# Stick-breaking attention taken two heads at a time, with the mask added ahead of the softplus

## The reference, cut to what matters

```python
z = einsum('bqhd,bshd->bhqs', qb, k) * HEAD_DIM ** -0.5
before = pos[None, :] < pb[:, None]                 # key position below query position
log_one_minus = where(before, log_sigmoid(-z), 0.0)
log_stick = cumsum(log_one_minus, axis=3, reverse=True) - log_one_minus
a = where(before, exp(log_sigmoid(z) + log_stick), 0.0)
o = einsum('bhqs,bshd->bqhd', a, v)
y = (o * silu(g)) @ w_out
```

## Time and profile before

| | |
|---|---|
| time, median of 3 executions | 1088.21 us (1086.91 to 1091.32) |
| span of the profiled execution, first to last instruction | 1090.5 us |
| PE busy | 1050.6 us (96%) |
| DVE, ACT, POOL busy | 700.0, 539.2, 226.2 us (64%, 49%, 21%) |
| PE's mean granted clock | 0.982 of 2.4 GHz |
| DMA | 173.28 MB, mean 159 GB/s |
| first logits product (L581) to first product of `ob` (L361) | 328.80 to 374.94 us |

### The profile page before, as it was taken

How to read it: one execution, slowest core, us unless ns; L and a number is a source line. 1 busy time by engine, 2 the same in 40 slices (tenths; PEclk the granted TensorE clock), 3 DMA queues, 4 the chain that set the end, 5 groups by cost and what they waited for, 6 DMA issues and landing times.

```text
span 1090.5 us, 19954 instructions
## 1 busy us (share of the span) xinstructions
PE 1050.6 (96%) x8160; PEld 1012.0 (93%) x8160; DVE 700.0 (64%) x1002; ACT 539.2 (49%) x822; POOL 226.2 (21%) x167
## 2 busy tenths in 40 slices
PE   8969999999999999999999999999999999999996
PEld 8969986999998899979999999999999999999996
DVE  5989976674446567635555657845566655657843
ACT  4335556355548636445435436644345545436641
POOL 3745201220003423000100202521015100202520
PEclk9889999999999999999999999989999999999998
DMA  9334530646542153624452545446545452545431
GB/s 344 114 117 151 194 116 1 232 154 231 189 161 76 65 192 118 245 102 155 172 174 79 194 158 189 154 166 254 198 171 201 173 188 80 193 159 188 154 116 39
DMA packets 26624, 173.28 MB, mean 159 GB/s; under 512 B 2880, under 2 KB 5184, under 8 KB 5952
## 3 DMA queue, kind: packets, MB, share of 16 engines
q1 hardware_dynamic: 24832, 161.26, 41.4%
q10 hardware_dynamic: 1728, 11.14, 2.6%
HBM read 167.15 MB, written 5.24 MB: 158 GB/s over the span
## 4 chain that ended last, share of the span: by engine, by line
PE 76%; DVE 11%; ACT 5%; POOL 2%; issue 2%; DMA 1%; SPq 0%; POOLq 0%; DVEq 0%; ACTq 0%
PE bank L361 64%; DVE wl L1142 4%; PE bank L467 3%; PE bank L494 2%; DVE work L1453 2%; ACT wh L718 2%; DVE work L1172 2%; DMA vec<-vecs 1%; POOL acc L1579 1%; PE bank L483 1%; DVE work L1456 1%; PE bank L429 1%; PE bank L581 1%; ACT work L1063 1%; PE bank L645 1%
## 5 line engine op out<-in xcount | busy, mean ns | idle before, releaser
L1142 DVE TENSOR_TENSOR wl<-raw,wh 128x1024 fp32r<-128x1024 f32 x300 | 394.6, 1323 | 250.8 <-ACT wh L718 248.9
L718 ACT ACTIVATE wh<-raw 128x1024 fp32r<-128x1024 f32 x300 | 312.9, 1054 | 307.1 <-PE bank L361 289.5
L361 PE MATMUL bank<-xh,wh 128*128 128x256 f32 x1312 | 368.5, 288 | 7.7 <-DVE wl L1142 5.7
L361 PE MATMUL bank<-xh,wl 128*128 128x256 f32 x1312 | 363.8, 284 | 0.0
L361 PE MATMUL bank<-xl,wh 128*128 128x256 f32 x1312 | 340.0, 284 | 0.0
L361 PEld LDWEIGHTS bank<-xh,wh 128*128 128x128 f32 x1312 | 253.2, 193 | 9.1 <-DVE wl L1142 8.1
L361 PEld LDWEIGHTS bank<-xh,wl 128*128 128x128 f32 x1312 | 253.3, 193 | 0.2
L361 PEld LDWEIGHTS bank<-xl,wh 128*128 128x128 f32 x1312 | 238.7, 193 | 0.1
L361 PE MATMUL bank<-yh,wh 128*128 128x256 f32 x768 | 212.3, 289 | 0.9 <-ACT yh L1067 0.9
L361 PE MATMUL bank<-yh,wl 128*128 128x256 f32 x768 | 210.1, 286 | 0.0
L361 PE MATMUL bank<-yl,wh 128*128 128x256 f32 x768 | 180.8, 286 | 4.2 <-POOL yl L1614 4.2
(11 more groups left out here) (154 smaller groups left out, 1320.8 us busy)
## 6 DMA issues: line engine op xcount, KB each, us to landing
raw<-w SPq DMA_DIRECT2D x149, 1024.0 KB, 4.8
k_scratch<-kt ACTq DMA_DIRECT2D x2, 1024.0 KB, 7.2
kt<-k_scratch ACTq DMA_DIRECT2D x2, 1024.0 KB, 6.3
cs<-cst SPq DMA_DIRECT2D x1, 1152.0 KB, 13.0
raw<-w SPq DMA_DIRECT2D x2, 512.0 KB, 5.8
h<-xt SPq DMA_DIRECT2D x1, 1024.0 KB, 6.1
v<-memt ACTq DMA_DIRECT2D x1, 1024.0 KB, 8.3
m_scratch<-yh ACTq DMA_DIRECT2D x1, 1024.0 KB, 4.3
```

The source lines that it names most:

```text
L361: return pe.matmul(b[:, j, :], lhs, rhs, start=k0 + k == 0 and q == 0 and (j == 0 or not both_open), stop=k0 + k == KT * p.deep - 1 and q ...
L718: act.activation(wh[:, n % 2, :, part], raw[:, n % RAW_SLOTS, :, part], ACT.Copy).then_inc(hi_ready, 1)
L1142: dve.tensor_tensor(wl[:, n % 2, :, part], raw[:, n % RAW_SLOTS, :, part], wh[:, n % 2, :, part].bitcast(F32), ALU.subtract).then_inc(lo_r ...
```

## The change

The change does seven things.

1. The logits use 64 rows of the array: `kt[r, g, ...]` and `qz[r, a, ...]` with r the 64 partitions of the head, instead of 128 rows with zeros. The two heads of a pair are issued alternately, each into a bank of its own, and four banks are used in turn instead of two.
2. The three value products of a pair are issued alternately too: first part of both heads, second of both, third of both. They are issued once both heads' Exp is done.
3. TensorE's program goes by pairs: scores of pair g, values of pair g-2, sums of the two heads of pair g-1. Its waits for the banks and for the copy of `v` stand ahead of the scores of pair 1. The hook in `vb` issues the scores of pair 0 together, and the second hook is gone.
4. VectorE adds the mask of -1e30 to the logits first (`z_first`), for a head as soon as its logits are there. ScalarE's Abs reads that masked tile from SBUF and waits for it.
5. The softplus is made from the masked tile (`z_soft` on VectorE), so that a masked place gives 0 by itself. GpSimd's multiplication goes, and the mask of ones and zeros goes from the table of constants: 384 of 2304 columns of 128 x 4 bytes, 192 KB.
6. ScalarE's Exp of the exponent takes head t-4 in step t instead of t-3, VectorE's exponent head t-4 instead of t-2, and the gates have a lag of 8.
7. GpSimd's low parts follow one another with nothing between.

```diff
-            def z_scores(a):
-                if a >= 2:
-                    pe.wait_ge(z_neg, a - 1)
-                b = bank[4 + a % 2]
-                pe.matmul(b[:, 0:S], kt[:, a // 2, 0:P], qz[:, a, :], start=True, stop=True)
-                pe.matmul(b[:, S:S + P], kt[:, a // 2, LATE], qz[:, a, LATE], start=True, stop=True).then_inc(z_full, 1)
+            zbank = [bank[4], bank[5], bank[PH["vb"].pair], bank[PH["vb"].pair + 1]]
+            def head_rows(a):
+                return slice(HD * (a % 2), HD * (a % 2) + HD)
+            def z_scores(g):
+                if g >= 2:
+                    pe.wait_ge(z_neg, 2 * g - 2)
+                for a in (2 * g, 2 * g + 1):
+                    r = head_rows(a)
+                    pe.matmul(zbank[a % 4][:, 0:S], kt[r, g, 0:P], qz[r, a, :], start=True, stop=True)
+                for a in (2 * g, 2 * g + 1):
+                    r = head_rows(a)
+                    pe.matmul(zbank[a % 4][:, S:S + P], kt[r, g, LATE], qz[r, a, LATE],
+                              start=True, stop=True).then_inc(z_full, 1)
...
-            project("vb", xh, xl, tok=True, hooks={(3, 0, 3): first_logits, (3, 1, 3): lambda: z_scores(1)})
+            project("vb", xh, xl, tok=True, hooks={(3, 0, 3): first_logits})
...
-                pe.wait_ge(z_masked, a + 1)
+                pe.wait_ge(z_sp, a + 1)
...
-            def z_values(a):
-                pe.wait_ge(z_prob, a + 1)
...
+            def z_values(g):
+                pe.wait_ge(z_prob, 2 * g + 2)
+                if g >= 2:
                     pe.wait_ge(dve_evac, pb.base + g - 1)
...
+                for b, pr, cols in heads:
+                    pe.matmul(b[:, 0:P], v[:, 0, cols], pr[:, 0:P], start=True, stop=True)
+                for b, pr, cols in heads:
+                    pe.matmul(b[:, P:S], v[:, 0, cols], pr[:, P:S], start=True, stop=False)
+                for b, pr, cols in heads:
+                    pe.matmul(b[:, P:S], v[:, 1, cols], pr[:, S:S + P], start=False, stop=True).then_inc(o_full, 1)
+            enter(pb)
+            pe.wait_ge(act_evac, PH["vb"].end)
+            for g in range(1, NH // 2 + 2):
+                if g < NH // 2:
+                    z_scores(g)
+                if g >= 2:
+                    z_values(g - 2)
+                if g < NH // 2 + 1:
+                    z_sums(2 * g - 2)
+                    z_sums(2 * g - 1)
...
             def z_soft(t):
 
                 z = wk(t % 2)[:, 0:ZW]
-                act.wait_ge(z_full, t + 1)
+                act.wait_ge(z_neg, t + 1)
                 if t >= 2:
                     act.wait_ge(z_sp, t - 1)
-                act.activation(z, bank[4 + t % 2][:, 0:ZW], ACT.Abs).then_inc(z_abs, 1)
+                act.activation(z, wk(4 + t % 4)[:, 0:ZW], ACT.Abs).then_inc(z_abs, 1)
...
-            for t in range(NH + 5):
-                if 2 <= t < NH:
+            for t in range(2, NH + 7):
+                if t < NH:
                     z_soft(t)
-                if 3 <= t < NH + 3:
-                    a = t - 3
+                if 4 <= t < NH + 4:
+                    a = t - 4
                     pr = wk(8 + a % 2)[:, 0:ZW]
                     act.wait_ge(z_arg, a + 1)
                     act.activation(pr, pr, ACT.Exp).then_inc(z_prob, 1)
-                gated_high("B", pb, t, 6)
+                gated_high("B", pb, t, 8)
...
+            def z_first(t):
+                dve.wait_ge(z_full, t + 1)
+                if t >= 4:
+                    dve.wait_ge(z_arg, t - 3)
+                dve.tensor_tensor(wk(4 + t % 4)[:, 0:ZW], zbank[t % 4][:, 0:ZW], c_("beforeneg"),
+                                  ALU.add).then_inc(z_neg, 1)
+            def z_soft(t):
                 dve.wait_ge(z_ln, t + 1)
                 if t >= 2:
+                    dve.wait_ge(c_full, t - 1)
+                dve.wait_ge(z_neg, t + 1)
+                dve.scalar_tensor_tensor(wk(2 + t % 2)[:, 0:ZW], wk(4 + t % 4)[:, 0:ZW], 0.0, wk(t % 2)[:, 0:ZW],
+                                         ALU.max, ALU.add).then_inc(z_sp, 1)
+            def z_exponent(a):
+                dve.wait_ge(c_full, a + 1)
+                if a >= 2:
+                    dve.wait_ge(o_full, OBASE["B"] + 2 * (a // 2))
+                dve.tensor_tensor(wk(8 + a % 2)[:, 0:ZW], wk(4 + a % 4)[:, 0:ZW], bank[6 + a % 2][:, 0:ZW],
+                                  ALU.subtract).then_inc(z_arg, 1)
...
+            chunks("vb", middle=first_z, hold=True)
+            for t in range(2, NH + 7):
+                if 4 <= t < NH + 4:
+                    z_exponent(t - 4)
                 if t < NH:
-                    z_step(t)
+                    z_first(t)
+                if t < NH + 2:
+                    z_soft(t - 2)
                 zgate(t)
...
-            for t in range(NH + 6):
-                if t < NH:
-                    pool.wait_ge(z_sp, t + 1)
...
-                    pool.tensor_tensor(wk(4 + t % 2)[:, 0:ZW], wk(2 + t % 2)[:, 0:ZW], c_("before"),
-                                       ALU.mult).then_inc(z_masked, 1)
-                if t >= 6 and t % 2 == 0:
-                    gated_low("B", (t - 6) // 2)
+            for g in range(8):
+                gated_low("B", g)
```

More of the change, by code:

```diff
@@ L56 @@
 _at = 0
-for _name, _n in (("ident", 128), ("cos", 256), ("sin", 256), ("adm", 512), ("before", 384), ("beforeneg", 384),
+for _name, _n in (("ident", 128), ("cos", 256), ("sin", 256), ("adm", 512), ("beforeneg", 384),
                   ("tri", 128), ("colneg", 256)):
@@ L265, in build @@
         z_full, z_abs, z_ln, z_sp = sem("z_full"), sem("z_abs"), sem("z_ln"), sem("z_sp")
-        z_masked, z_neg, c_full, z_arg, z_prob = sem("z_masked"), sem("z_neg"), sem("c_full"), sem("z_arg"), sem("z_prob")
+        z_neg, c_full, z_arg, z_prob = sem("z_neg"), sem("c_full"), sem("z_arg"), sem("z_prob")
         f_full, f_copied = sem("f_full"), sem("f_copied")
@@ L600, in z_sums @@
                 pe.matmul(b[:, S:S + P], tri, sp_[:, S:S + P], start=True, stop=True).then_inc(c_full, 1)
-            def z_values(a):
-                pe.wait_ge(z_prob, a + 1)
-                g = a // 2
-                if a % 2 == 0 and g >= 2:
+            def z_values(g):
+                pe.wait_ge(z_prob, 2 * g + 2)
+                if g >= 2:
                     pe.wait_ge(dve_evac, pb.base + g - 1)
[L607 to L613, removed]
-                if t < NH:
[L615 to L622, removed]
+                heads = [(bank[pb.pair + g % 2][head_rows(a)], wk(8 + a % 2), slice(HD * a, HD * a + HD))
+                         for a in (2 * g, 2 * g + 1)]
+                for b, pr, cols in heads:
[14 more added lines that the diff above has]
+                    z_sums(2 * g - 1)
             project("ob", yh, yl, y_ready("B", g_lo, GBASE["B"], 1))
@@ L1379, in _ @@
             ZW = S + P
-            zgate = gated("B", PH["attB"], 5)
-            def z_step(t):
-                b = bank[4 + t % 2][:, 0:ZW]
+            zgate = gated("B", PH["attB"], 8)
+            zbank = [bank[4], bank[5], bank[PH["vb"].pair], bank[PH["vb"].pair + 1]]
+            def z_first(t):
[4 more added lines that the diff above has]
+                                  ALU.add).then_inc(z_neg, 1)
@@ L1385, in z_step @@
+            def z_soft(t):
                 dve.wait_ge(z_ln, t + 1)
                 if t >= 2:
[L1387 to L1393, removed]
-                dve.tensor_tensor(wk(6 + t % 2)[:, 0:ZW], b, c_("beforeneg"), ALU.add).then_inc(z_neg, 1)
@@ L1396, in _ @@
-            chunks("vb", middle=lambda c: z_step(0) if c == 3 else None, hold=True)
-            for t in range(1, NH + 5):
-                if 2 <= t < NH + 2:
-                    a = t - 2
-                    dve.wait_ge(c_full, a + 1)
-                    if a >= 2:
-                        dve.wait_ge(o_full, OBASE["B"] + a - 1)
-                    dve.wait_ge(z_neg, a + 1)
-                    dve.tensor_tensor(wk(8 + a % 2)[:, 0:ZW], wk(6 + a % 2)[:, 0:ZW], bank[6 + a % 2][:, 0:ZW],
-                                      ALU.subtract).then_inc(z_arg, 1)
+                    dve.wait_ge(c_full, t - 1)
@@ L1406, in _, with first_z @@
+            def first_z(c):
+                if c == 3:
+                    z_first(0)
+                    z_first(1)
+            chunks("vb", middle=first_z, hold=True)
+            for t in range(2, NH + 7):
+                if 4 <= t < NH + 4:
+                    z_exponent(t - 4)
                 if t < NH:
-                    z_step(t)
+                    z_first(t)
+                if t < NH + 2:
+                    z_soft(t - 2)
                 zgate(t)
@@ L1701, in tables @@
     before = np.concatenate([p[:, None] < s[None, :], p[:, None] < p[None, :]], 1)
-    put("before", before.astype(np.float32))
     put("beforeneg", np.where(before, 0.0, NEG))
```

6 lines of the change are left out of this document (1 added, 5 removed).

## The result

The changed kernel takes 1126.08 us (median of 4, 1124.23 to 1129.29) against 1089.18 us before (median of 4, 1086.91 to 1091.32): a ratio of 1.034, 95% interval 1.032 to 1.036. It is slower by 37 us, and the forecast of 1132 us stands 6 us above it.

A forecast was written before the change was run, and what follows sets the result against it. TensorE was taken to bound the kernel, 5.09 us a pair of heads in the stick-breaking layer. 1088.2 + 25.5 (loop) + 19.5 (clock) - 0.5 (table) = 1132.7, so 1132 us; 8 in 10 for 1110 to 1148.

The forecast's parts named there:

- The loop: Stick-breaking layer: TensorE's values wait for an Exp behind `z_soft(2g+1)`; 8.8 us a turn, 9.2 with copy; layer grows 25.5 us.
- The clock: Same layer: TensorE idles about 5 us every turn, so each round begins at 1.2 GHz; 19.5 us lost.
- The draining rounds: Layer's end: two rounds drain behind ScalarE's step 14 (386.8), `ob` starting at 400.4; half clock adds 4.9 us.
- the start of the loop: Layer's beginning: from first logits at 328.80 to ScalarE in step 4 at 341.6; scores of pair 1 start 1.2 us later.
- The row halves: TensorE's scores: 64-row halves taken to overlap in full, by the column halves' trace row; 0.65 us a pair, not 1.29.
- the second rival: Scores: row halves don't overlap, 0.43 us more in each of 8 rounds, and clock stays down in the layer; 1145, 20%.
- The start: Kernel's start, where VectorE waits for the table of constants: the table shrinks by 192 KB, saving 0.5 us.
- The signs: Profile after: layer about 72 us, TensorE idle about 5, ScalarE over 4 before every second Abs, clock near 0.6 or 0.7.
- The warm one: Stick-breaking layer: the loop closes, but the clock stays up; 1113, 15%.
- The one with no overlap: Scores in the layer: row halves don't overlap and the clock stays down; 1132 + 13 = 1145, 20%.
- the fast one: Layer: engines work ahead and work alone counts; ScalarE's 4.25 us a pair sets the pace; 1082, 3%.

The follow-up runs named there:

- the clock held up: 20 needless 128-column products put behind the scores of pairs 2 to 7 where TensorE would idle, against the changed kernel; 1113.37 us, ratio 1.022.
- the last kernel: Logits on all 128 rows again, against the kernel with order opened and a ring of six buffers; 1083.68 us, ratio 0.9965.
- the kernel with all loops open and half rows both: Changed kernel with order opened on three engines, exponent and Exp in place in six buffers, copy of `v` early; 1081.54 us, ratio 0.994.

## Why the prediction was right, point by point

**The loop.** It was the main step, and it holds as written: the wait of the values on the Exp, the Exp behind `z_soft(2g+1)`, and that behind the scores. With the clock held up the turns were 8.89 and 9.20 us; the sums said 8.8 and 9.2. ScalarE's leg took 341.67 to 345.65, 3.98 us for 3.95. TensorE idled 5.18 to 5.49 us ahead of the values for "about 5".

**The clock.** It fell in every turn, as said. In the kernel the turns were 11.12, 10.70, 10.65, 12.05 and 11.21 us, 11.15 on average; my terms come to (2 x 8.8 + 3 x 9.2) / 5 + 2.45 = 11.5. By the granted clock it came back 4.8, 3.9, 3.1, 6.1 and 4.3 us after the work had resumed, and half of each (2.4, 2.0, 1.6, 3.1, 2.2) is close to what its turn was longer than 8.89 or 9.20 (2.2, 1.8, 1.5, 2.9, 2.0). I had taken 4.9 from a single case. The mechanism was right, the size a sixth too large (2.45 for 2.1). One argument for it was misread: "three of three idle times above 2 us" leaves out two of the kernel before. TensorE idled 2.12 us ahead of 1038.50, and the clock fell to 0.50; it idled 2.06 us ahead of 8.37, and the clock stayed at 1.00. Nor is 2 us a limit: in the changed kernel the clock was at 0.50 from 337 us on, behind idle times of 1.34 and 1.08 us.

**The draining rounds.** This is the term that was mis-sized. From step 14 to `ob` I had 13.6 us, and 5.6 more for half clock throughout. It took 412.59 - 397.40 = 15.2 us. Ahead of the last two values TensorE idles for 1.57 and 1.20 us only, and the clock, back at 405 us, stayed up. `ob` started at full pace, so its 1.8 us weren't lost either. Together 5.8 us too much. The layer took 85.4 us where my terms gave 71.6 + 17.7 = 89.3; the draining rounds make 4 us of the difference, the turns 1.7, and the start of the loop took 1.6 us more than said (14.4 us from the first logits to step 4 instead of 12.8), as the clock was at half from 337 us on, one round earlier than I had it. That forecast and measurement are 6 us apart is in part luck: 7.5 us too much (drain 4.0, turns 1.7, `ob` 1.8) against 1.6 too little at the start, and slow stretches of the clock elsewhere that are no part of the sum.

**The row halves.** Taken as overlapping in full by the nearest row, and so they did. Their worth on the loop was 0.24 us a turn, not the 0.43 that the second rival had: the price was for the pair, and the loop leaves with the first head. The Trainium skill, "TensorEngine Tiling (Array Packing)", in its section on theoretical speedup, gives up to twice the rate for such halves. The rows bear that out for the passes (0.54 us for four, change of shape included, against 0.87 on 128 rows), and the time says that it decides little while the loop is closed.

**The start.** The table's 192 KB were put at 0.5 us. The load lands after 12.6 us where it took 13.0, so 0.4 of that is borne out for the load itself:

```profile
cs<-cst SPq DMA_DIRECT2D x1, 960.0 KB, 12.6
```

What it is worth in time can't be told: the kernel with the mask alone gives 0.1% less, with an interval that holds zero. In the profile the layer began 1.6 us earlier and what follows the layer was 5.5 us shorter (710.1 us for 715.6), because three slow stretches of the clock at 414, 712 and 1039 us don't occur in it. No run ties either to the change: the waits in front of two of these stretches, 2.12 us each for `yl`, are there in the profile after as well, and there the clock stayed at 1.00.

**The signs.** The prediction said that the layer would last about 72 us; that is its 71.6 without the clock, and its own terms with the clock give 89.3. ScalarE idled for 6.4 to 7.8 us before every second Abs ("over 4"), but released by the softplus, L1410, and not by `z_first`; the sum had this right, with the softplus last in VectorE's leg. The granted clock was 0.74 for "0.6 or 0.7". The logits' passes start in pairs, as said: two of the four lie within the 0.13 us from 350.72 to 350.85.

**The rivals.** The warm one (1113) is what the run with needless products gives, 1113.37, with its condition, a loop closed at full clock. The one with no overlap (1145) fell by its rows, the fast one (1082) by the order; though once its condition was met by another order, the time was 1081.54, and the pace was ScalarE's work, 4.25 us a pair, as that rival said.

## What to carry to other kernels

When work is regrouped, follow the order of each engine's program around one full turn before adding up the work: if a wait on one engine stands ahead of the instruction that the releasing engine needs, directly or two engines on, the legs add up instead of overlapping, and less work takes more time. Opening one such loop shows the next, down to the number of buffers, so draw all of them, with the buffer reuse, before moving an instruction. And an idle TensorE is paid for twice, in the wait and in the half clock behind it; needless products in the wait, if they end before the wait does, are a quick test of how much is which.

## What the runs showed of the hardware that was not expected

The first RoPE multiplication on VectorE waits for the constants. In nine of the twelve profiles with the smaller table it started at 18.6 to 18.7 us, in three at 20.0 to 20.2, with the same loads in the same order; the kernel before had it at 20.35 in its one profile. Two of them, the one after and that with the mask alone:

```profile
18.56 0.68 DVE L1186 TENSOR_TENSOR work<-work,cs 32x512 f32<-32x512 f32 x1 [0.46 <-DMA vec<-vecs]
```

```profile
20.07 2.37 DVE L1172 TENSOR_TENSOR work<-work,cs 32x512 f32<-32x512 f32 x2 [2.04 <-DMA vec<-vecs]
```

In the kernel before and in two of the three late ones TensorE's clock was then at 0.50 from about 39 to 46 or 48 us; with the early start it stayed at 1.00 there every time, and was at 0.50 for part of 55 to 65 us. Executions of one kernel fall in two heaps some 4 us apart (1083 and 1087.7 us in the last kernel's twelve), but these are not the early and the late starts: that kernel's profiled execution took 1087.22 us, in the upper heap, and started early, at 18.64.

One thing that differs between profiles is whether the clock falls behind the same wait. The last kernel's profile and that of the kernel with all loops open and half rows both have an idle time of 0.94 us on TensorE followed by eight one-column products, near 226 us. In the last kernel's profile the granted clock was then at 0.50 from 229 to 231 us; in the other it stayed at 1.00. And the wait of 2.12 us for `yl` near the end of the span lowered the clock in the kernel before, and not in the changed one. So the length of such an idle time alone doesn't settle what the clock does, and which executions make up the upper heap stays open.

The last is that halves of the rows overlap with plain float32 operands too, whose products stand in the records as two passes: four passes of 256 columns take 0.54 us from the first start to the next line's, and 0.87 us on all 128 rows.
